# Gating products of the plain pairs on GpSimd, and a reordered hand-over from plain slots to blocks, in a two-layer encoder kernel

## The reference

```python
def conv_gated_mlp(h, w_up, conv_w, conv_b, w_down):
    up = h @ w_up                                   # 1024 -> 2 * 2816
    half = CONV_W // 2
    pad = jnp.pad(up, ((0, 0), (half, half), (0, 0)))
    conv = sum(pad[:, j:j + s] * conv_w[j] for j in range(CONV_W)) + conv_b
    a, b = jnp.split(conv, 2, axis=-1)
    return (jax.nn.gelu(a) * b) @ w_down

x = x + conv_gated_mlp(rmsnorm(x, g_ffn[l]), w_up[l], conv_w[l], conv_b[l], w_down[l])
```

## Time and profile before

| What | us |
|---|---|
| median of 3 runs | 1685.12 (1685.02 to 1685.22) |
| the profiled execution | 1685.78 |
| its span, first to last instruction | 1684.0 |
| TensorE busy in the span | 1671.1 |
| VectorE busy | 1015.5 |
| ScalarE busy | 844.4 |
| GpSimd busy | 824.0 |

### The profile page before, as it was taken

One profiled execution on the slowest core, in us unless ns is written; L12 is line 12 of the kernel. 1 busy time (PEld: TensorE's weight loads), 2 busy tenths in 40 slices (PEclk: granted clock), 3 DMA queues, 4 the chain that ended last, 5 costly groups with the idle time before them and its releaser, 6 DMA issues.

```text
span 1684.0 us, 24393 instructions
## 1 busy us (share of the span) xinstructions
PE 1671.1 (99%) x9017; PEld 1449.9 (86%) x9017; DVE 1015.5 (60%) x1652; ACT 844.4 (50%) x1533; POOL 824.0 (49%) x808
## 2 busy tenths in 40 slices
PE   9999999999999999999999999999999999999998
PEld 7888888888887999988888888888888879999886
DVE  4768876533339867661246788656333598666642
ACT  4666654223245666662256667432223556666322
POOL 3444332433356688844344334324233568888432
PEclk9999999999999999999999999999999999999999
DMA  7422222223332333342352222332342422333422
GB/s 253 135 76 76 76 101 101 77 98 121 128 135 91 101 101 101 102 162 94 100 193 86 90 76 76 100 100 75 100 149 94 144 88 101 101 101 101 163 95 81
DMA packets 147320, 182.78 MB, mean 109 GB/s; under 512 B 3040, under 2 KB 130706, under 8 KB 146194
## 3 DMA queue, kind: packets, MB, share of 16 engines
q1 hardware_dynamic: 147090, 181.35, 32.1%
q10 hardware_dynamic: 128, 0.09, 0.0%
HBM read 170.92 MB, written 10.50 MB: 108 GB/s over the span
## 4 chain that ended last, share of the span: by engine, by line
PE 95%; DVE 2%; POOL 1%; ACT 1%; issue 1%; ACTq 0%; POOLq 0%
PE banks L1851 17%; PE banks L1852 17%; PE banks L1853 17%; PE banks L2087 6%; PE banks L2092 6%; PE banks L2088 6%; PE banks L1886 3%; PE banks L1887 3%; PE banks L1888 3%; PE banks L2166 2%; PE banks L2168 2%; PE banks L2167 2%; PE banks L1915 2%; PE banks L1942 2%; POOL w_lo L630 1%; PE banks L2017 1%
## 5 line engine op out<-in xcount | busy, mean ns | idle before, releaser
L630 POOL TENSOR_TENSOR w_lo<-raw,w_hi 128x256 fp32r<-128x256 f32 x616 | 495.5, 839 | 740.1 <-ACT w_hi L731 740.1
L1851 PE MATMUL banks<-xg_hi,w_hi 128*128 128x512 f32 x832 | 325.6, 391 | 2.7 <-POOL w_lo L630 2.7
L1852 PE MATMUL banks<-xg_lo,w_hi 128*128 128x512 f32 x832 | 324.3, 390 | 0.0
L1853 PE MATMUL banks<-xg_hi,w_lo 128*128 128x512 f32 x832 | 323.8, 389 | 0.0
L1278 DVE TENSOR_TENSOR w_lo<-raw,w_hi 128x768 fp32r<-128x768 f32 (+2 forms) x114 | 100.9, 885 | 174.0 <-ACT w_hi L730 173.8
L1851 PEld LDWEIGHTS banks<-xg_hi,w_hi 128*128 128x128 f32 x832 | 156.3, 188 | 35.0 <-POOL w_lo L630 3.5
L1853 PEld LDWEIGHTS banks<-xg_hi,w_lo 128*128 128x128 f32 x832 | 156.2, 188 | 32.9
L1852 PEld LDWEIGHTS banks<-xg_lo,w_hi 128*128 128x128 f32 x832 | 156.4, 188 | 31.0 <-issue 0.2
L730 ACT ACTIVATE w_hi<-raw 128x768 fp32r<-128x768 f32 (+2 forms) x115 | 84.0, 730 | 177.4 <-PE banks L1853 90.8
L731 ACT ACTIVATE w_hi<-raw 128x1280 fp32r<-128x1280 f32 (+3 forms) x115 | 153.7, 1336 | 0.0
L672 POOL TENSOR_TENSOR a_lo<-raw,a_hi 128x1024 fp32r<-128x1024 f32 x64 | 119.8, 1872 | 52.9 <-ACT a_hi L1041 52.9
(11 more groups left out here) (239 smaller groups left out, 3954.8 us busy)
## 6 DMA issues: line engine op xcount, KB each, us to landing
raw<-in_w_in SPq DMA_DIRECT2D x55, 1024.0 KB, 5.0
raw<-in_w_up SPq DMA_DIRECT2D x44, 1024.0 KB, 5.0
raw<-in_w_br SPq DMA_DIRECT2D x16, 1024.0 KB, 5.0
raw<-in_w_down SPq DMA_DIRECT2D x12, 1024.0 KB, 5.0
x_spill<-x_res SPq DMA_DIRECT2D x4, 2048.0 KB, 7.4
x_res<-x_spill SPq DMA_DIRECT2D x4, 2048.0 KB, 9.6
raw<-in_w_out SPq DMA_DIRECT2D x8, 1024.0 KB, 5.0
raw<-in_w_down SPq DMA_DIRECT2D x8, 896.0 KB, 4.6
```

The lines of the kernel that those rows point to most:

```text
L630: last = nc.gpsimd.tensor_tensor(w_lo[p_][:, k, :], raw[p_][:, k, :], f32(w_hi[p_][:, k, :]), ALU.subtract)
L1851: nc.tensor.matmul(out, w_hi[w][:, k, cols], x_hi[:, a, :], start=first and k == 0, stop=False)
L1852: nc.tensor.matmul(out, w_hi[w][:, k, cols], x_lo[:, a, :], start=False, stop=False)
L1853: mm = nc.tensor.matmul(out, w_lo[w][:, k, cols], x_hi[:, a, :], start=False, stop=last and k == kt - 1)
```

## The change

Four edits, in each of the two layers:

1. VectorE no longer makes the gating products of the plain pairs (six for each layer).
2. GpSimd makes them: those of pair 0 ahead of its split of slot S_F+3, those of pair 1 ahead of and behind its split of slot S_F+5, those of pair 2 behind `block_lo(0,0)` and behind `block_lo(0,2)`. The function `multiply` is the one that GpSimd has already, with its waits for the second tap of the convolution and for the gelu.
3. GpSimd's `operand_lo(5)` moves from behind the split of S_F+2 to behind the split of S_F+3.
4. ScalarE's `conv_centre(5,1)` moves from ahead of `seed(0,0)` to behind `seed(0,1)`.

```diff
@@ -671,12 +671,6 @@
                 pool.wait_ge(s_hi, 4 * Z + (1, 3, 3, 4)[n])
                 nc.gpsimd.tensor_tensor(out, src, f32(hi), ALU.subtract).then_inc(s_lo, 1)
 
-            for s in range(S_F + 2, S_S):
-                split(s)
-                for q in {S_F + 2: (5,), S_F + 4: (4, 6)}.get(s, ()):
-                    operand_lo(q)
-            for n in range(4):
-                block_lo(0, n)
             def multiply(z, half):
                 i = (NS + z) // 2
                 pool.wait_ge(conv2_ok, conv_n(l, z, half))
@@ -684,6 +678,21 @@
                 nc.gpsimd.tensor_tensor(g_f32[:, 2 * i + half, :].rearrange("p (r n) -> p r n", r=REQS), act[half][:, :, :],
                                         conv_of(z, half), ALU.mult).then_inc(gated_ok, 1)
 
+            for s in range(S_F + 2, S_S):
+                if s == S_F + 3:
+                    multiply(1 - NS, 0)
+                    multiply(1 - NS, 1)
+                if s == S_F + 5:
+                    multiply(3 - NS, 0)
+                split(s)
+                if s == S_F + 5:
+                    multiply(3 - NS, 1)
+                for q in {S_F + 3: (5,), S_F + 4: (4, 6)}.get(s, ()):
+                    operand_lo(q)
+            for n in range(4):
+                block_lo(0, n)
+                if n in (0, 2):
+                    multiply(-1, n // 2)
             for z in range(1, SZ):
                 for n in range(4):
                     block_lo(z, n)
@@ -1102,11 +1111,12 @@
                         block_centre(z - 1, half)
                 else:
                     block_hi(1, 0)
-                    conv_centre(NS - 1, 1)
                 seed(z, 0)
                 if 0 < z < SZ - 1:
                     block_hi(z + 1, 0)
                 seed(z, 1)
+                if z == 0:
+                    conv_centre(NS - 1, 1)
                 if z < SZ - 1:
                     block_hi(z + 1, 1)
                     if z:
@@ -1641,8 +1651,6 @@
                     if (n, half) == (NS - 1, 0):
                         block_low(0)
                     convolve(n - NS, half, up_bank(n, half).rearrange("p (r n) -> p r n", r=REQS))
-                    if n % 2:
-                        multiply(n - NS, half)
                     if (n, half) == (NS - 1, 0):
                         evacuate(NS - 1, 1)
                         block_adds(1)
```

## The result

The changed kernel takes 1692.84 us (median of 6, 1691.23 to 1693.99) where the kernel before takes 1685.28 (6, 1685.02 to 1685.62): a ratio of 1.004, 95% interval 1.003 to 1.005. So it is slower by 7.6 us where +6.7 was forecast; the time lies 1.0 us above the 1691.8 of the forecast and inside the range. The execution that was profiled took 1693.09 us, its span is 1691.3.

The account below looks back on a forecast made before the run. TensorE was taken as the bound, its two repeated holes (5.0 us) all there was to win; the late z = 2 load adds 3.8 in layer 0 and 2.9 in layer 1, +6.7 on 1685.12: 1691.8 us, range 1689 to 1695.

Parts of the forecast that it names:

- Hole 1 closes: TensorE in slot S_F+3, before the fourth weight tile: the 1.5 us wait for GpSimd's w_lo goes, in each layer.
- Hole 2 closes: TensorE before product 2 of block 0: the 1.0 us wait for ScalarE's first seed goes, in each layer.
- the first rival: Whole kernel: both holes close in both layers and nothing takes their place, 5.0 us won, 1680.1 us; chance 7%.
- The convolution of (5,0) comes 0.5 us earlier: Layer 0, ahead of multiply(-1,0): ends at 561.6 instead of 562.09, taken from a possible 0 to 3.4 us earlier.
- SP issues at 569.9: SP's load for z = 2, layer 0: issued at 569.9 in place of 564.33, 5.6 us later.
- Landing 5.0 to 6.5: Load for z = 2, issue to arrival: 5.0 us (median of 44) to 6.5, so stage(2) runs at 574.9 to 576.4.
- `seed(1,0)` 1.96 us behind `stage(2)`: ScalarE's queue: 1.96 us of work from stage(2) to seed(1,0), 3.06 before; 1.1 us of waiting goes.
- `seed(1,2)`, +0.6: Block 1: seed(1,2) comes 3.51 us behind seed(1,0), TensorE needs 2.9 us from product 2 to product 4: +0.6 us.
- the third rival: TensorE after the new wait: clock drops to 1.2 GHz, products take 2.9 us instead of 1.45; 1697.6 or 1706 us; chance 8%.
- That VectorE is freed ... is worth nothing by itself: VectorE, twelve products moved away: the 12 x 0.84 = 10 us freed wins nothing by itself.
- costs nothing: GpSimd, slot S_F+3: h_low ends 3 to 5 us later, free because its first user is block 0's product 5.
- the split S_F+5: GpSimd's split behind one 1.4 us product ends near 549.4, wanted at 550.6: no wait, or up to 1 us.

Follow-up runs that it names:

- e1: Changed kernel with GpSimd's pair 2 products moved behind all of block 0 and behind block_lo(1,0): 1680.41 us, ratio 0.9966 to the kernel before.
- e5: Kernel before, with SP waiting for two more s_lo before loading over block 0's raw, no product moved: 1695.33 us, ratio 1.0055.
- e2: Kernel before with the two reorderings alone (operand_lo(5) and conv_centre(5,1)), all gating products staying on VectorE: 1686.45 us, ratio 1.0004.
- e3: Kernel before with only pair 2's products moved to GpSimd, at the change's places, neither queue reordered: 1696.01 us, ratio 1.0063.
- e4: Changed kernel plus ten identity transposes on TensorE in block 1's wait, leaving part of a sum out of the output: 1691.09 us, ratio 1.003.
- e8: Changed kernel plus ten identity matmuls on TensorE in block 1's wait, adding into a region nothing reads: 1690.42 us, ratio 1.0029.
- e7: Changed kernel with only pair 2's second product moved behind block_lo(0,3), the first left in place: 1688.38 us, ratio 1.0017.

## Why the prediction was right

The mechanism was the one on record: pair 2's products ahead of `block_lo(0,3)` make the load for z = 2 late, and the two closed holes vanish into the wait for it. e1 takes this away and gets both holes back; e5 makes the load late without any product and loses no less. But that the total came out within 1 us is luck: two errors of size went against each other, a load that was priced too long and a fall of the clock that was left out. One of the prediction's own signs of being wrong did come, the granted clock below 1.00; and two of its signs of being right came with other sizes, TensorE standing still for 2.83 and 3.08 us and not 3 to 5, and SP's issue 6.7 us later against block 0 (9.96 and 3.29), since block 0 itself began 1.6 us earlier. Times of after are set on before's by the 0.59 us by which its slot S_F of layer 0 began earlier.

- *Hole 1 closes*: forecast 1.5 us, P is 1.60 shorter. Right. *Hole 2 closes*: nothing is left before product 2 of block 0. Right. That they "do not come off": right, and e1 shows what they are worth when they do (with VectorE freed, see e2), 5.2 us against the 5.0 of the first rival.
- *The convolution of (5,0) comes 0.5 us earlier*, 561.6: its product began at 560.77, which is 561.36. The size was right, the reason only in part. VectorE's `s` of block 0 took 2.70 us beside GpSimd's `a_lo`, but it had taken 2.59 before; most of the freed time was gone ahead of it, for VectorE's first sum of block 0 began only 0.90 us earlier (551.15, which is 551.74, and 552.64 before). On the way VectorE had waited 0.51 and 0.63 us for TensorE, and one `h_t` beside GpSimd's `h_low` had taken 3.48 us (526.97) in place of 1.21. Had pairs 0 and 1 stayed on VectorE, this would have been worse: in e3 the product begins 0.61 us later against slot S_F's start.
- *SP issues at 569.9*: 568.81, which is 569.40. The chain was 0.5 us too long, as a product took 1.30 and not 1.4 and the first began 0.24 us earlier.
- *Landing 5.0 to 6.5*: this is the mis-sized term. ScalarE's wait ended 4.95 us behind the issue in layer 0, where I gave that layer the 6.5 of rows 5 and 8. One row is a single transfer; the median of 44 was the better price. In layer 1 of before ScalarE's same wait ended with VectorE's `s_lo`, not with the load, so the 6.5 was not a rule even there.
- *`seed(1,0)` 1.96 us behind `stage(2)`*: 1.86. So product 2 of block 1 came 1.70 us later in layer 0 and 2.00 in layer 1 (B and P together), below the +2.3 to +3.8.
- *`seed(1,2)`, +0.6*: 579.14 is 3.52 us behind `seed(1,0)`; e4 and e8, where the clock doesn't cover it, show +0.51 in C.
- These alone make 2.2 + 2.5 = 4.7 us, so 1689.8; e8, with the clock held, has +4.9. The missing 3.2 us are the third rival, held at 8%: the clock does fall after the wait, in both layers. Its price, 2.9 us a layer for two products, was right for a product (2.70 and 2.55 us in layer 0 for 1.44), but in layer 1 only one was slow throughout (2.57). The chance was too low: the wait that was forecast was longer than either hole in the trace of before, and rows at 1.00 beside holes of 1.35 us say nothing of one of 3. And "No row of this trace has a granted clock under 1.00" does not hold at the end of the trace of before, behind TensorE's last matmul at 1677.11:

```profile
1682.00:1684.00 2.00, 0.00 (x0) 0.00 (x0) 0.00 (x0) 0.00 (x0) 0.00 (x0) 0.64 0.53 215
```

Three sentences were wrong. "That VectorE is freed ... is worth nothing by itself" fell with e2: once the two holes are closed by order alone, VectorE is next, at S_F+5 and in block 0, and its twelve products are worth 6.0 us. The forecast asked what ends the holes that show, and not what comes close behind. That the move of `operand_lo(5)` "costs nothing" looked only at who uses `h_low`; e2's timeline has it make VectorE 0.7 us later. And the split S_F+5 was costed as if only GpSimd's share of it could be late; in e2 it is VectorE's.

A rule of the Trainium skill was weighed for the third rival: "TensorE: Matmul & The Clock Gate", section "Why this matters for your kernels", holds that a long enough gap between bursts of matmuls brings the slow clock back. The changed kernel's trace agrees: 0.50 after idle times of 2.83 and 3.08 us.

## What to carry to other kernels

When work goes to a queue that is in order, look at what else that queue releases: here two products of 1.30 us stood ahead of the last instruction that frees a load's buffer, and behind that instruction they cost nothing. An engine that nobody waits for today may be close behind the one that is; before writing its relief down as nothing, ask who is late once the visible hole is closed, and whom the moved work will now run beside. And a wait of 1.9 to 3.7 us on TensorE had, in most cases here, a second price in what runs after it, which ten spare matmuls in the wait took away when the wait itself stayed.

## What was not expected of the hardware

*The clock does not follow the length of the last wait alone.* The granted clock fell after waits of 2.83 and 3.08 us (the changed kernel), 3.67 and 2.93 (e5), 2.98 (e3, layer 1), and 1.86 (e7, layer 1), which came behind shorter waits of 0.56 and 0.28 us in the same blocks. It did not fall after 1.57 (e7, layer 0, behind 0.53 and 0.28), not after 1.85 and 1.86 in e4, where the ten transposes had run ahead of what was left of the wait, and not after 2.92 us in e3, layer 0, though e3 had four shorter waits ahead of it:

```profile
582.00:584.00 2.00, 1.61 (x13) 1.65 (x14) 1.97 (x3) 2.00 (x5) 0.75 (x2) 1.00 0.34 88
...
1420.00:1422.00 2.00, 2.00 (x14) 2.00 (x13) 1.96 (x3) 2.00 (x4) 1.40 (x1) 0.67 0.75 238
```

These are e3's stretches behind the two waits, the first at 1.00 and the second at 0.67. What decides between two waits of nearly one length was not tried, and stays open.

*Who gets in first is worth a microsecond.* e3 and e5 shortened P by 1.1 us with no edit in it. The instructions of slot S_F+3 are those of before, but GpSimd's five `w_lo` took 5.25 us in e5 and 6.29 before, and the hole was 0.29 us and not 1.35. VectorE's `h_t`, with two operands in SBUF, runs beside them; GpSimd's and VectorE's timelines of e5:

```profile
523.81 5.25 POOL L630 TENSOR_TENSOR w_lo<-raw,w_hi 128x256 fp32r<-128x256 f32 x5
```

```profile
528.31 1.83 DVE L1568 TENSOR_TENSOR h_t<-h,h 128x1024 f32<-128x1024 f32 x1
```

Before, the same `h_t` began at 528.46 and took 1.21 us: there VectorE was first and the fifth `w_lo` waited, in e5 GpSimd was first and `h_t` waited. The same is seen in e3's `s` of 2.95 us against 0.69. So the hole that the change set out from was partly an accident of order. The Trainium skill, "SBUF — State Buffer", section "Who interferes with whom", has a VectorE instruction with two SBUF inputs contend with a GpSimd instruction that reads SBUF, over ports that it calls an exclusive lock. The traces agree: 1.83 us in place of 1.21, 2.95 in place of 0.69.
